# HGRN2 head sums: squared outputs as the moving operand, the rows turned back by four transposes

## The chip, the cores and the metric

The kernel runs on one core of one Trainium2 chip. The metric is the device time of one execution in microseconds (us), median of the runs. The core has a matrix engine (TensorE, PE in the profile, with its weight loads as PEld), VectorE (DVE), ScalarE (ACT), GpSimd (POOL) and SyncE (SP), each with an instruction queue of its own that it works off in order; they wait for each other on semaphores. TensorE writes to PSUM, eight banks of 128 partitions x 512 fp32 values.

## The reference

A trunk of two layers on x of shape (1, 512, 1024), fp32. Each layer is a half-step SwiGLU FFN, a mixer, and a second half-step FFN; a final RMSNorm closes it. The mixer projects the normed input with one matrix W_in, and runs two token mixers side by side, a Mamba-2 SSD head group and an HGRN2 head group, whose outputs W_out joins. The change lies in the norm of the HGRN2 outputs, one for each of the 8 heads of 64 values and each of the 512 tokens:

```
o = (o_intra + o_inter).reshape(Bsz, L, HG_HEADS, HG_VAL_HEAD)
o = o * lax.rsqrt(jnp.mean(o * o, axis=-1, keepdims=True) + NORM_EPS) * norm_w
o = o * jax.nn.silu(g_raw.reshape(Bsz, L, HG_HEADS, HG_VAL_HEAD))
```

So the kernel needs 512 x 8 sums, each over the 64 squares of a head.

## The kernel before, in words

Channels lie on the 128 partitions and the 512 tokens along the free dimension (four tiles of 128 tokens, c = 0 to 3). Large products are made from a high and a low part: for each 128x128 weight block three matmuls of 512 columns (L1215 to L1217, `products`), with the high part of the weights rounded by ScalarE (`whi`) and the low part subtracted by GpSimd (`wlo`, L418). Weight blocks come by DMA from SP into four slots.

In the mixer TensorE goes through the list PROJ, blocks n = 0 to 26 of W_in: f, B, dt, C, then q and i of four head pairs, g0, then xs and z of four head pairs in turn (n = 16 is xs0, 17 z0, 18 xs1, 19 z1, 20 xs2), and g1 to g3. Each block is eight products (k = 0 to 7), that is 24 matmuls, into bank n % 3. The small matmuls of the two mixers are written by hand between the products and behind the blocks. VectorE copies each block out (`evac`) and does most of the elementwise work, ScalarE the exponentials, tanh and squares. The order on each engine is that of the code; there is no planner.

Around the change the order is as follows.

- TensorE: behind the products of n = 18 come the SSD state contributions of pair 0 (`ssd_contribs`, L1461) and `head_sums` (L1491), into bank 7. Then the 24 products of n = 19, then `ssd_outs(0)` (L1477, L1482), which overwrites bank 7 and so waits for `head_norm`, `ssd_turn(1)` (L1445 to L1451), and block n = 20.
- VectorE: `evac(18)` (L812), the convolution of xs1 (L868, L871), its SiLU (L825), `ssd_states(0)` (L1028, L1034), then the wait for `head_sum` and `rsqrt` (L659 to L668), eleven small steps on 128x32 values, the first reading bank 7 and the last signalling `head_norm`. Behind it comes `evac(19)` (L819).
- `head_spreads` (behind n = 20, 22 and 24) uses `rh`, the result, in which tokens lie on partitions and c and head (8c + head) along the free dimension.

In `head_sums` each of the 16 products has a 128x128 tile of squares `km` as its stationary operand and the table `headsum` (128x8 for each head pair p, ones where a channel belongs to a head) as the moving one: 8 columns for each token tile c, accumulated over four pairs.

`acb`, an 8x512 tile, holds the running sums of the SSD decay. Its last reads are in the blocks up to n = 8 (the transposes of `common`, and the splitting into `acb_hi` and `acb_lo`, L1108 and L1110).

Of the kernel before, what the change touches and what calls it, by code (L numbers as in the profile page):

```python
# [23 lines left out]
NP = 4  # L24
# [94 lines left out]
def trunk_kernel(nc, x_in, cols, first_norm, logits, lead, up1, dn1, mix, dtw, up2, dn2, out):  # L119
    ctx = ExitStack()  # L120
    with ctx:
# [3 lines left out]
        def ev(name, per=0, before=0, credit=0):  # L125
            return Event(ctx.enter_context(nc.semaphore(name)), per, before, credit)
# [42 lines left out]
        ident = sb("ident", [P, P])  # L169
# [67 lines left out]
        def bank(i):  # L237
            return ps[:, i, :]
# [70 lines left out]
        o_done = ev("o_done", NP)  # L309
        o_out = ev("o_out", 2 * NP)  # L310
        head_sum = ev("head_sum", 1)
        head_norm = ev("head_norm", 1)
        head_spread = ev("head_spread", NP)
        head_used = ev("head_used", NP)
# [334 lines left out]
        def _(dve):  # L649
# [103 lines left out]
            with dve.Fori(0, DEPTH) as l:  # L753
# [6 lines left out]
                def ready(e, k=0):  # L760
                    dve.wait_ge(e.sem, e.upto(l, k))
# [320 lines left out]
                for n, (kind, pr) in enumerate(PROJ):  # L1082
                    evac(n)
                    if n == 10:
                        ready(cleared)
                    if n == 5:
                        dt_first()
                    if n in (1, 2, 4, 5):
                        gate_f((1, 2, 4, 5).index(n))
                    if kind in ("B", "C"):  # L1090
                        convolve(kind, n)
                    if n == 3:
                        conv_out("B")
                    if kind == "C":
                        dt_rest()
                        conv_out("C")
                        for p in range(NP):
                            scan_f(p)
                    if n == Q0:
                        hg_dist(0)  # L1100
                        hg_q(0)
                    if n == Q0 + 1:
                        dt_out()
                        hg_k(0)
                        hg_tables()
                        hg_levels(0)
                        cb_mask()
                        did(dve.tensor_copy(acb_hi[:], acb[:]))  # L1108
                        settle()
                        made(acb_split, tt(acb_lo[:], acb[:], acb_hi[:].bitcast(F32), ALU.subtract))  # L1110
                    if n in (9, 11, 13):
                        p = (n - 9) // 2
                        if p == 0:
                            ends()
                        hg_dist(p + 1)
                        hg_q(p + 1)
                    if n in (10, 12, 14):
                        p = (n - 10) // 2
                        if p == 0:
                            end_weights()  # L1120
                        hg_mask(p)
                        hg_states(p)
                        hg_k(p + 1)
                        hg_levels(p + 1)
                    if n == 15:
                        ready(proj_out, n)
                        silu(("g", 0), g2[:, 0, :], gs[:, 0, :])
                    if kind == "xs":
                        if pr == 0:
                            hg_mask(3)  # L1130
                            hg_states(3)
                        convolve(pr, n)
                        conv_out(pr)
                        if pr:
                            ssd_states(pr - 1)
                        if pr == 1:
                            ready(head_sum)
                            rsqrt(head_norm, rh, None, bank(7)[:, 0:TC * 8], 1.0 / HALF)
                        if pr == 2:
                            hg_norm(0, 3)  # L1140
                            hg_gate(0)
                            hg_lo(0)
                        if pr == 3:
                            hg_norm(1, 3)
                            group_rsqrt(0)
                    if kind == "z":
                        ready(proj_out, n)
                        silu(("z", pr), g2[:, 0, :], zs[:, pr % 2, :])
                        if pr:
                            ssd_gate(pr - 1)  # L1150
                        ssd_main(pr)
                    if kind == "g" and pr in (1, 2):
                        ready(proj_out, n)
                        silu(("g", pr), g2[:, 0, :], gs[:, pr % 2, :])
                        if pr == 1:
                            ssd_states(3)
                        hg_gate(pr)
                        if pr == 1:
                            ssd_norm(0)
                            ssd_norm(1)  # L1160
                            hg_norm(2, 3)
                            hg_norm(3, 4)
                            hg_lo(1)
                        else:
                            ssd_lo(0)
                            ssd_lo(1)
                            hg_lo(2)
                            ssd_gate(3)
# [30 lines left out]
        def _(pe):  # L1199
# [41 lines left out]
            with pe.Fori(0, DEPTH) as l:  # L1241
                def ready(e, k=0):
                    pe.wait_ge(e.sem, e.upto(l, k))
# [72 lines left out]
                def cols_of(c):  # L1316
                    return slice(c * P, (c + 1) * P)
# [100 lines left out]
                def hg_outs_before_ready(p):  # L1418

                    ready(state, p)  # L1420
                    ready(level, 6 * p + 5)
# [64 lines left out]
                def head_sums():  # L1486

                    ready(o_out, 2 * NP - 1)
                    for c in range(TC):
                        for p in range(NP):  # L1490
                            last = mm(bank(7)[:, 8 * c:8 * c + 8], km[:, p, cols_of(c)], headsum[:, 8 * p:8 * p + 8],  # L1491
                                      start=p == 0, stop=p == NP - 1)
                    last.then_inc(head_sum.sem, 1)

                def head_spreads(p, bk):

# [25 lines left out]
                for i, (n, k0, k1) in enumerate(PBLOCKS):  # L1522
                    w = MIX0 + i
                    ready(split, w)
                    if k0 == 0:
                        ready(proj_out, n - 3)
                    for k in range(k0, k1):
                        norm_steps(1, n, k)
                        if n in (10, 12, 14, 16) and k == SCORES_FROM:
                            hg_scores_ready((n - 10) // 2)  # L1530
                        if n in (11, 13, 15, 17) and k == 6:
                            hg_outs_before_ready((n - 11) // 2)
                        last = products(bank(n % 3), w % NS, k - k0, h_tile(k), k == 0, k == KD - 1)
                        if k == k1 - 1:
                            last.then_inc(blk.sem, 1)

                        if n in (10, 12, 14, 16):
                            for c in SCORES_AT[k]:
                                hg_scores((n - 10) // 2, c)
                        if n in (11, 13, 15, 17) and k == 4:  # L1540
                            hg_outs_inside((n - 11) // 2)
                        if n in (11, 13, 15, 17) and k == 6:
                            hg_outs_before((n - 11) // 2)
                    if k1 < KD:
                        continue
                    if n == 8:
                        common()
                    if n == 9:
                        chunk_ends()
                    if n in (9, 11, 13, 15):  # L1550
                        hg_turn((n - 9) // 2)
                    if n in (10, 12, 14, 16):
                        hg_contribs((n - 10) // 2)
                    if n in (19, 21, 23, 25):
                        ssd_outs((n - 19) // 2)
                    if n in (17, 19, 21, 23):
                        ssd_turn((n - 17) // 2)
                    if n == 22:
                        group_sums(0)
                    if n in (18, 20, 22, 24):  # L1560
                        ssd_contribs((n - 18) // 2)
                    if n == 18:
                        head_sums()
                    if n == 20:
                        head_spreads(0, 3)
                    if n == 22:
                        head_spreads(1, 3)
                    if n == 24:
                        head_spreads(2, 3)
                        head_spreads(3, 4)  # L1570
                        group_spreads(0)
# [112 lines left out]
```

## Time and profile before

| | |
|---|---|
| time, median of 3 runs | 2055.16 us (2054.82 to 2055.25) |
| the profiled execution: time | 2053.32 us |
| its span, first to last instruction | 2051.6 us |
| mean granted clock of TensorE | 0.983 of full speed |
| TensorE busy | 1999.3 us (97%), 10684 matmul records |
| VectorE busy | 811.8 us (40%) |
| ScalarE busy | 660.1 us (32%) |
| GpSimd busy | 850.7 us (41%) |
| DMA | 181.66 MB, mean 89 GB/s |

Busy time is the time in which an engine worked on some instruction. TensorE's matmuls are pipelined, so the distance between the starts of two of them says more than the duration of one. A plain fp32 matmul leaves two records in the profile, a transpose or one of the three matmuls of a product leaves one. The granted clock is the share of TensorE's full 2.4 GHz that the chip gave; it has two levels, 1.0 and 0.5. The mixer of layer 1 lies between about 390 and 620 us of the span, that of layer 2 between about 1400 and 1630 us, and the head sums at 539 and 1547 us.

### The profile page before, as it was taken

How to read it: one execution, taken by the hardware profiler on the slowest of the kernel's cores; microseconds unless marked ns; L12 is line 12 of the kernel's file. 1: busy time of each engine (PE TensorE's matmuls, PEld its weight loads, DVE VectorE, ACT ScalarE, POOL GpSimd, SP SyncE). 2: the span in 40 equal slices, each digit the busy share in tenths (PEclk: the TensorE clock that was granted, in tenths of full speed). 3: DMA queues.
4: the chain of work that ended last, by engine and by line, in shares of the span. 5: the costliest groups of instructions: out<-in, count | busy, mean ns of one | idle time of the engine just before them, and what ended most of it. 6: DMA issues, size and time to landing. Idle time of an engine off the chain costs nothing.

```text
span 2051.6 us, 29158 instructions
## 1 busy us (share of the span) xinstructions
PE 1999.3 (97%) x10684; PEld 1640.8 (80%) x10684; DVE 811.8 (40%) x1274; ACT 660.1 (32%) x903; POOL 850.7 (41%) x362
## 2 busy tenths in 40 slices
PE   8999999979999999999999999999799999999999
PEld 6888888867778888888888888888577788888888
DVE  7222211597786322221142222117868762222112
ACT  4323222343443232323232322224334332322222
POOL 4544445442224344444434444444322244444453
PEclk9999999989999999999999999999899999999998
DMA  4322233221112232233322223322111122223332
GB/s 145 113 100 95 88 104 95 83 73 53 53 61 83 82 102 92 96 93 95 106 94 92 100 93 95 95 87 93 52 63 52 52 93 94 100 93 100 95 94 91
DMA packets 55816, 181.66 MB, mean 89 GB/s; under 512 B 8369, under 2 KB 10417, under 8 KB 55729
## 3 DMA queue, kind: packets, MB, share of 16 engines
q1 hardware_dynamic: 55728, 180.52, 27.1%
q8 instruction: 52, 0.85, 0.2%
q14 instruction: 36, 0.29, 0.0%
HBM read 178.40 MB, written 2.10 MB: 88 GB/s over the span
## 4 chain that ended last, share of the span: by engine, by line
PE 87%; DVE 9%; issue 3%; ACT 1%; DMA 0%; SPq 0%; DVEq 0%; ACTq 0%
PE ps L1215 28%; PE ps L1216 27%; PE ps L1217 27%; DVE acc L832 1%; PE ps L1374 1%; DVE xs L871 1%; DVE lm L1022 0%; DVE b L835 0%; PE ps L1415 0%; PE ps L1491 0%; ACT th L491 0%; PE ps L1230 0%; DVE b L839 0%; DVE t L830 0%; DVE g L819 0%
## 5 line engine op out<-in xcount | busy, mean ns | idle before, releaser
L418 POOL TENSOR_TENSOR wlo<-raw,whi 128x1024 fp32r<-128x1024 f32 x348 | 848.4, 2440 | 1190.0 <-ACT whi L451 626.9
L1215 PE MATMUL ps<-hhi,whi 128*128 128x512 f32 x1840 | 730.5, 397 | 0.0
L1216 PE MATMUL ps<-hlo,whi 128*128 128x512 f32 x1840 | 720.8, 392 | 0.0
L1217 PE MATMUL ps<-hhi,wlo 128*128 128x512 f32 x1840 | 720.5, 392 | 0.0
L1215 PEld LDWEIGHTS ps<-hhi,whi 128*128 128x128 f32 x1840 | 348.9, 190 | 79.8 <-issue 7.2
L1217 PEld LDWEIGHTS ps<-hhi,wlo 128*128 128x128 f32 x1840 | 348.2, 189 | 73.9
L1216 PEld LDWEIGHTS ps<-hlo,whi 128*128 128x128 f32 x1840 | 348.7, 190 | 70.1
L451 ACT ACTIVATE whi<-raw 128x1024 fp32r<-128x1024 f32 x168 | 177.4, 1056 | 358.5 <-PE ps L1217 358.5
L1215 PE MATMUL ps<-ahi,whi 128*128 128x512 f32 x704 | 273.9, 389 | 0.0
L1216 PE MATMUL ps<-alo,whi 128*128 128x512 f32 x704 | 273.9, 389 | 0.0
L1217 PE MATMUL ps<-ahi,wlo 128*128 128x512 f32 x704 | 273.9, 389 | 0.0
L784 DVE TENSOR_TENSOR u<-ps,r 128x512 f32<-128x512 f32 x88 | 60.8, 691 | 387.1 <-PE ps L1217 387.1
L457 ACT ACTIVATE whi<-raw 128x1024 fp32r<-128x1024 f32 x176 | 183.8, 1045 | 28.2 <-PE ps L1217 28.2
L470 ACT ACTIVATE ahi<-u 128x512 f32 (+1 forms) x88 | 55.6, 632 | 405.9 <-DVE u L787 405.9
L794 DVE SCALAR_TENSOR_TENSOR x<-ps,x 128x512 f32<-128x512 f32 x32 | 22.1, 692 | 387.4 <-PE ps L1217 387.4
L1215 PEld LDWEIGHTS ps<-ahi,whi 128*128 128x128 f32 x704 | 132.1, 188 | 27.6
L1216 PEld LDWEIGHTS ps<-alo,whi 128*128 128x128 f32 x704 | 132.1, 188 | 27.4
L1217 PEld LDWEIGHTS ps<-ahi,wlo 128*128 128x128 f32 x704 | 132.1, 188 | 27.3
L466 ACT ACTIVATE g<-g 128x512 f32<-128x512 f32 x88 | 55.5, 631 | 238.7 <-DVE g L782 238.7
L782 DVE TENSOR_TENSOR g<-ps,r 128x512 f32<-128x512 f32 x88 | 60.8, 691 | 177.4 <-PE ps L1217 176.5
L789 DVE TENSOR_TENSOR alo<-u,ahi 128x512 f32 x88 | 63.5, 722 | 83.7 <-ACT ahi L470 83.7
L433 ACT ACTIVATE hhi<-x,par 128x512 fp32r<-128x512 f32 x48 | 34.5, 719 | 150.9 <-DVE x L794 141.6
(225 smaller groups left out, 1389.6 us busy)
## 6 DMA issues: line engine op xcount, KB each, us to landing
raw<-in_up SPq DMA_DIRECT2D x168, 512.0 KB, 3.2
raw<-in_mix SPq DMA_DIRECT2D x66, 512.0 KB, 3.2
raw<-in_dn SPq DMA_DIRECT2D x64, 448.0 KB, 3.3
raw<-in_dn SPq DMA_DIRECT2D x32, 512.0 KB, 3.5
raw<-in_lead SPq DMA_DIRECT2D x12, 512.0 KB, 3.3
stage<-in_x SPq DMA_DIRECT2D x4, 512.0 KB, 7.0
out<-stage SPq DMA_DIRECT2D x8, 256.0 KB, 2.6
raw<-in_mix SPq DMA_DIRECT2D x4, 256.0 KB, 2.5
```

The costliest lines, as they stand in the source:

```text
L418: pool.tensor_tensor(wlo[:, q, :], raw[:, q, :], whi[:, q, :].bitcast(F32), ALU.subtract).then_inc(split.sem, 1)
L433: act.activation(hhi[:, m, :], x[:, m, :], ACT.Copy, scale=gain).then_inc(x_high.sem, 1)
L451: act.activation(whi[:, q, :], raw[:, q, :], ACT.Copy).then_inc(high.sem, 1)
L457: act.activation(whi[:, q, :], raw[:, q, :], ACT.Copy).then_inc(high.sem, 1)
L466: act.activation(g2[:, jj, :], g2[:, jj, :], ACT.Silu).then_inc(silu_g.sem, 1)
L470: act.activation(ahi[:, 2 * i + jj, :], u2[:, jj, :], ACT.Copy).then_inc(hid_high.sem, 1)
L782: made(g_out, tt(g2[:, jj, :], bank(jj), r[:], ALU.mult))
L784: made(u_out, tt(u2[:, jj, :], bank(2 + jj), r[:], ALU.mult))
L789: made(hid_low, tt(alo[:, 2 * i + jj, :], u2[:, jj, :], ahi[:, 2 * i + jj, :].bitcast(F32), ALU.subtract))
L1215: mm(dst, whi[:, q, s], mh, start=start, stop=False)
L1216: mm(dst, whi[:, q, s], ml, start=False, stop=False)
L1217: return mm(dst, wlo[:, q, s], mh, start=False, stop=stop)
```

## The change

The operands of the head sums change places: `headsum` (128x8 for each pair) is the stationary operand and `km`, all 512 tokens of a pair, the moving one. Four products instead of 16 accumulate into rows 0 to 7 of bank 7: heads on partitions, tokens along the free dimension. VectorE copies these 8x512 values to `acb` and signals `head_rows`. TensorE waits for that in block n = 19 ahead of the products k = 3, and behind these products turns the rows by four transposes of 8x128 into bank 7, in the layout of before (`head_turned`). VectorE waits for them and goes on with `rsqrt` as before.

```diff
+        head_rows = ev("head_rows", 1)
+        head_turned = ev("head_turned", 1)
...
                         if pr == 1:
                             ready(head_sum)
+                            made(head_rows, dve.tensor_copy(acb[:], bank(7)[0:8, :]))
+                            ready(head_turned)
                             rsqrt(head_norm, rh, None, bank(7)[:, 0:TC * 8], 1.0 / HALF)
...
                 def head_sums():
 
                     ready(o_out, 2 * NP - 1)
+                    for p in range(NP):
+                        last = mm(bank(7)[0:8, :], headsum[:, 8 * p:8 * p + 8], km[:, p, :],
+                                  start=p == 0, stop=p == NP - 1)
+                    last.then_inc(head_sum.sem, 1)
+
+                def head_turn():
+
                     for c in range(TC):
-                        for p in range(NP):
-                            last = mm(bank(7)[:, 8 * c:8 * c + 8], km[:, p, cols_of(c)], headsum[:, 8 * p:8 * p + 8],
-                                      start=p == 0, stop=p == NP - 1)
-                    last.then_inc(head_sum.sem, 1)
+                        last = pe.transpose(bank(7)[:, 8 * c:8 * c + 8], acb[:, cols_of(c)], ident[0:8, 0:8])
+                    last.then_inc(head_turned.sem, 1)
...
+                        if n == 19 and k == 3:
+                            ready(head_rows)
                         last = products(bank(n % 3), w % NS, k - k0, h_tile(k), k == 0, k == KD - 1)
                         if k == k1 - 1:
                             last.then_inc(blk.sem, 1)
+                        if n == 19 and k == 3:
+                            head_turn()
```

## Rows read from the trace of the kernel before

**Rows 1.** The page, part 4: the chain that ended last, by engine.
```profile
PE 87%; DVE 9%; issue 3%; ACT 1%; DMA 0%; SPq 0%; DVEq 0%; ACTq 0%
```

**Rows 2.** The chain of waits, layer 1: start us, us, what.
```profile
539.07 3.75 PE ps L1491 x32
...
544.30 0.43 PE ps L1215
...
558.89 0.24 PE ps L1217
```

**Rows 3.** Timeline of TensorE, layer 1: start us, us, engine, line, operation.
```profile
538.20 0.87 PE L1461 MATMUL ps<-xde,bt 128*64 128x128 f32 x6
539.00 3.82 PE L1491 MATMUL ps<-headsum,km 128*128 128x8 f32 x32
542.68 0.78 PE L1215 MATMUL ps<-hhi,whi 128*128 128x512 f32 x1
...
549.54 0.39 PE L1217 MATMUL ps<-hhi,wlo 128*128 128x512 f32 x1
```

**Rows 4.** Timeline of VectorE, layer 1; in brackets idle time before, and its releaser.
```profile
539.39 2.69 DVE L868 TENSOR_SCALAR xs<-xr,par 128x512 f32<-128x512 f32 x1
...
547.02 0.17 DVE L659 TENSOR_SCALAR ntn<-ps 128x32 f32<-128x32 f32 x1
...
550.06 0.69 DVE L819 SCALAR_TENSOR_TENSOR g<-ps,r 128x512 f32<-128x512 f32 x1 [0.61 <-PE ps L1217]
...
557.73 1.28 DVE L1022 TENSOR_TENSOR lm<-lm,cbm 128x512 f32<-128x512 f32 x2
...
559.89 0.55 DVE L868 TENSOR_SCALAR xs<-xr,par 128x512 f32<-128x512 f32 x1
```

**Rows 5.** Timeline of TensorE, layer 2.
```profile
1546.73 4.55 PE L1491 MATMUL ps<-headsum,km 128*128 128x8 f32 x32
...
1558.88 0.39 PE L1217 MATMUL ps<-hhi,wlo 128*128 128x512 f32 x1
```

**Rows 6.** Timeline of VectorE, layer 2.
```profile
1554.74 0.18 DVE L659 TENSOR_SCALAR ntn<-ps 128x32 f32<-128x32 f32 x1
```

**Rows 7.** Stretches: start:end, us, TensorE busy (records), granted clock, DMA share, GB/s.
```profile
542.52:545.94 3.42, 3.42 (x10) 0.50 0.47 153
617.62:621.03 3.41, 3.41 (x10) 0.50 0.45 138
1549.45:1556.28 6.83, 6.83 (x22) 0.50 0.26 79
1624.55:1631.37 6.82, 6.82 (x25) 0.50 0.24 77
```

**Rows 8.** Operations from PSUM by line (ns min/median/max); transposes on the timeline of TensorE.
```profile
L703 DVE COPY r<-ps x6: 692/692/692, 41.0 to 1685.1; 128x512 f32<-128x512 f32 x6
...
L810 DVE TENSOR_TENSOR dtb<-ps,r x2: 671/672/672, 412.3 to 1420.7; 8x512 f32<-8x512 f32 x2
...
530.63 0.39 PE L1217 MATMUL ps<-hhi,wlo 128*128 128x512 f32 x1
530.86 0.60 PE L1445 MATMUL ps<-ident,xs 128*128 128x128 f32 x4
531.39 0.49 PE L1450 MATMUL ps<-acb_hi,identr 8*128 8x512 f32 x1
...
435.13 0.59 PE L1327 MATMUL ps<-ident,dtb 8*128 8x8 f32 x4
```

**Rows 9.** Waits of TensorE, 530 to 625 us (total, times, longest); one on the timelines.
```profile
PE ps L1477 <- DVE st L1034: 2.6, 2, 1.5
PE ps L1513 <- ACT sqb L491: 1.7, 1, 1.7
...
1575.84 0.96 DVE L1034 SCALAR_TENSOR_TENSOR st<-st,u,ps 64x64 f32<-64x64 f32 x4
...
1576.86 1.09 PE L1477 MATMUL ps<-lm,xdt 128*64 128x128 f32 x16 [1.06 <-DVE st L1034]
```

## The prediction

> **What bounds the kernel now.** I read the page first, then the chain of waits around the head sums, then the timelines of TensorE and VectorE there, in both layers. The page puts 87% of the chain of work that ended last on TensorE [rows 1], so the question in each stretch is whether TensorE may go on. In the chain of waits the sums themselves stand with 3.75 us, the products of block n = 19 (z1) behind them, and TensorE still at the last product of n = 20, which ends at 559.13 [rows 2]. So TensorE holds the end right through the place that is changed: whatever delays the last product of n = 19 delays everything behind it.
>
> The timeline of layer 1 [rows 3] gives the path. The 32 records of the sums start at 539.00, the 24 products of n = 19 run from 542.68 to 549.54 (last start). In layer 2 [rows 5] the sums start at 1546.73 and the last product at 1558.88. The granted clock is half (1.2 GHz) just behind the sums: for 3.4 us in layer 1 and 6.8 us in layer 2 [rows 7]. At that level successive 128x512 products are 0.43 us apart [rows 2], at 2.4 GHz 0.23 us (530.63 to 530.86 [rows 8]). That is why layer 2 needs longer for the same work.
>
> VectorE is the second path. In layer 1 it convolves block n = 18 (one pass of it takes 2.69 us), forms the SSD states and starts the head square root at 547.02, 4.4 us after TensorE had its sums ready (32 x 0.1117 us behind 539.00) [rows 3, 4]. The square root ends at 549.45, 0.61 us ahead of the next copy out at 550.06. In layer 2 the square root starts at 1554.74 [rows 6]. Today TensorE needs nothing of this before the end of n = 19, and its products fill the time.
>
> **The change part by part.** *The sums.* Before, 16 products give 32 records, 0.1117 us apart (3.57 us, to 542.57; the first product follows at 542.68) [rows 3]. After, four products of 512 columns give 8 records. No row shows a 512-column product of plain fp32. The nearest is the state contribution, fp32 with 128 columns: six records in 0.87 us, of which the last one's own 0.27 us run past the others' starts, so (0.87 - 0.27) / 5 = 0.12 us apart, 0.11 without the slower first [rows 3]; four times the columns make 0.44 us, and 8 records 3.5 us. The lower bound is the 0.23 us of a 512-column product of the other form, 8 x 0.23 = 1.8 us; the upper is the half clock, 7.0 us. I take 3.5 us: no gain to speak of in time. What may change is the clock, since the array now streams full-length operands instead of 8 columns.
>
> *The new wait.* TensorE waits for head_rows in front of the products k = 3 of n = 19. VectorE makes head_rows by a copy that stands, in its order, behind the convolution of n = 18 and behind the SSD states. It can't start before 547.02 in layer 1 and 1554.74 in layer 2, the present starts of the square root, since nothing ahead of it on VectorE depends on the sums. The copy reads 8x512 from PSUM. A 128x512 copy from PSUM takes 0.69 us and an 8x512 operation from PSUM 0.67 us [rows 8], so eight partitions are no cheaper than 128; the lowest bound is the 0.17 us of the 128x32 step [rows 4]. I take 0.69, and 0.06 us to wake TensorE (VectorE's states end at 1575.84 + 0.96 = 1576.80, the outputs that waited for them start at 1576.86 [rows 9]). TensorE goes on at 547.77 and 1555.49.
>
> When does it get there? In layer 1 at full clock: sums to 542.5, first product at 542.7, nine products (the first behind another kind of work takes 0.11 us more, 0.49 against 0.39 us [rows 8], so one pitch of 0.34, then 0.23) last start 544.65, streaming over at about 544.9. So it stands still for 2.9 us; the same sum gives 2.9 us in layer 2 (1546.73 + 3.5 + 0.2, nine products, 1552.6, against 1555.49). Behind the waiting product are 15 products of n = 19, and behind those the SSD outputs, the turning of x, and by way of the block's semaphore ScalarE's rounding of the next weights, GpSimd's subtraction and SP's next load. All move together; weights lie split ahead, so none of them is a new wait.
>
> *The four transposes.* Group L1445 shows what four transposes between long products cost: from the product at 530.63 to the one at 531.39 is 0.76 us, where 0.23 is usual, and the pitch after it is 0.34 instead of 0.23 [rows 8]. Together 0.64 us. The eight-row ones in the trace (x4 in 0.59 us, against 0.60) are not cheaper [rows 8].
>
> *End of n = 19.* Restart + 0.34 + 0.23 + 0.76 (over the transposes) + 0.34 + 10 x 0.23 = restart + 3.97 us. Layer 1: 547.77 + 3.97 = 551.74 against 549.54, **+2.2 us**. Layer 2: 1555.49 + 3.97 = 1559.46 against 1558.88, **+0.6 us** (it was already late, for its 6.8 us of half clock). Without the transposes and the copy the stall alone would still be there; they are not the cause but 0.64 + 0.69 us of it per layer.
>
> *The square root moves too.* It now starts when the transposes end, about 549.15, and needs 547.02 to 549.45 = 2.43 us [rows 4], so it ends at 551.6; the copy out of n = 19 would come at 551.74 + 0.52 = 552.26 (0.52 as from 549.54 to 550.06 [rows 3, 4]). That covers it by 0.65 us. If that cover goes, each further us is one on the path, as the SSD outputs wait for head_norm. Is the delay won back later? From the copy out of n = 19 (550.06) VectorE works, tied to that block by the tanh, until 559.0, and TensorE's last product of n = 20 ends at 559.13 [rows 2, 4]: both paths start at the end of n = 19 and are as long, so the delay goes through whole. Sum at full clock: **+2.8 us**.
>
> *The clock behind the stall.* In layer 1 TensorE stood idle for up to 1.5 us in front of the SSD outputs and the clock did not fall; it stood idle 1.7 us in front of the group sums, which are one-column products, and it fell for 3.4 us at 617.62; the like place of layer 2 has 6.8 us at 1624.55 [rows 7, 9]. The new stall of 2.9 us is longer than each of them, with five full products and four short transposes behind it. So I expect a fall. In a stretch of 3.4 us at the low level 8 products start where 15 would: 1.6 us lost, for each layer. The before times hold their own falls, since I compare with their real ends. The Trainium skill (Perfetto Trace Analysis, Matmul Optimizations) says that TensorE's power scales with utilization, so that matmuls should run back to back in batches. The falls above agree; by that rule the stall costs more than its length, and without it the sum would stay at the full-clock one.
>
> Sum with a fall in both layers: 2.8 + 2 x 1.6 = **+6.0 us**. The durations are of the profiled execution, 2053.32 us with a span of 2051.6; the median of the runs shown is 2055.16, 1.84 more, and I put the difference on the median: 2061.2 us.
>
> **The rivals.**
> 1. *A fall in one layer only.* Where the stall lies against the clock's decisions is chance, and an idle time of 1.5 us passed [rows 9]. +4.4 us: 2059.6.
> 2. *No fall behind the stall,* or the fall comes right behind the sums as now (eight columns of weights may count for as little as eight columns of data) and is spent in the nine products and the stall: nine at 0.43 us end by 546.6, still ahead of 547.77. +2.8 us: 2058.0. For it: both sums of before were followed by a fall [rows 7]. Against: there the data were 8 columns wide.
> 3. *Not slower: VectorE is early.* The long pass of the convolution in n = 18 takes 2.69 us beside a subtraction on GpSimd; the same pass in n = 20 takes 0.55 us [rows 4]. Should the two no longer meet, the copy starts 2.14 us sooner, TensorE restarts at 545.63 and 1553.35, and n = 19 ends at 549.60 and 1557.32: +0.06 - 1.56 = -1.5 us, 2053.7. It decides from 2.1 us on. The skill (Advanced Engine Details and Errata, VectorE Performance Modes) says that two-port VectorE instructions and GpSimd's block each other; the trace agrees (2.69 against 0.55). Against it: both instructions are released by the end of n = 18's products, ahead of the first changed instruction, in both layers.
> 4. *The long sums are slow* (half clock during and after, 7.0 us): TensorE reaches the wait at 546.2 + nine products at 0.43 = 550.1, 2.4 us behind 547.77, in both layers: 2.8 + 4.8 = +7.6, with a little of the low stretch behind it about +8.5: 2063.7.
>
> **How the numbers follow.** Fall in both layers 0.43, in one 0.27, none 0.19, VectorE early 0.05, slow sums 0.06. What a measurement of this kernel can tell from no change is 0.2%, 4.1 us: faster by more than that has no case of its own, only the last rival's sign with shifted clock stretches elsewhere (0.04); within 0.2% are the case without a fall, VectorE early, and a part of the one-fall case, whose +4.4 is at the edge (0.32); slower 0.64. Range: from 2058.0 less 1.0 (a copy of 0.17 us in both layers) to the slow-sum case: 2057.0 to 2063.8.
>
> **What would show it.** In the profile after: L1491's successor with 8 records of about 0.44 us; a stall of TensorE of 2 to 3 us in n = 19 released by VectorE's copy to acb, in both layers; the copy at 0.6 to 0.7 us starting at the time of today's first square-root step; the last product of n = 19 at +2.2 to +3.8 us in layer 1; half clock in the stretch after the stall. It would be wrong if TensorE doesn't wait for head_rows, if VectorE reaches its copy more than 2 us sooner, or if later stages take the delay up.

## The result, and the profile after

| | before | after |
|---|---|---|
| median | 2054.95 us (20 runs, 2050.59 to 2057.08) | 2058.27 us (20 runs, 2056.29 to 2065.32) |
| the profiled execution: time, span | 2053.32, 2051.6 us | 2065.32, 2063.6 us |
| granted clock in it | 0.983 | 0.982 |

The ratio is 1.0020, 95% interval 1.0013 to 1.0026: the change makes the kernel slower, by 2.7 to 5.3 us (the medians differ by 3.3). The profiled execution of the changed kernel is the slowest of its 20, so its span overstates the loss; its rows show the mechanism, the medians the size.

The page of the changed kernel. TensorE is still the chain; the new entry is in the last row: in front of the bracket are busy time and mean ns, behind it the idle time of TensorE before this line, 6.2 us, of which VectorE's write of `acb` ends 5.7.

```profile
span 2063.6 us, 29080 instructions
...
PE 86%; DVE 10%; issue 3%; ACT 1%; DMA 0%; SPq 0%; DVEq 0%; ACTq 0%
...
L1219 PE MATMUL ps<-hhi,whi 128*128 128x512 f32 x1840 | 732.2, 398 | 6.2 <-DVE acb L1140 5.7
```

TensorE in layer 1, the answer to [rows 2, 3] (start us, us, line, operation, in brackets idle time before and what ended it):

```profile
538.33 0.87 PE L1465 MATMUL ps<-xde,bt 128*64 128x128 f32 x6
539.13 3.60 PE L1494 MATMUL ps<-km,headsum 128*8 128x512 f32 x8
542.66 0.50 PE L1219 MATMUL ps<-hhi,whi 128*128 128x512 f32 x1
...
544.62 0.39 PE L1221 MATMUL ps<-hhi,wlo 128*128 128x512 f32 x1
547.87 0.50 PE L1219 MATMUL ps<-hhi,whi 128*128 128x512 f32 x1 [2.87 <-DVE acb L1140]
548.21 0.59 PE L1220 MATMUL ps<-hlo,whi 128*128 128x512 f32 x1
548.60 0.63 PE L1221 MATMUL ps<-hhi,wlo 128*128 128x512 f32 x1
549.16 0.59 PE L1501 MATMUL ps<-ident,acb 8*128 8x8 f32 x4
549.68 0.80 PE L1219 MATMUL ps<-hhi,whi 128*128 128x512 f32 x1
...
553.23 0.39 PE L1221 MATMUL ps<-hhi,wlo 128*128 128x512 f32 x1
553.55 1.09 PE L1481 MATMUL ps<-lm,xdt 128*64 128x128 f32 x16
```

The sums are 8 records in 3.60 us where 32 took 3.82, and the first product behind them starts at 542.66, before at 542.68. The whole stage lies 0.13 us later here. After nine products it stands still for 2.87 us. Then the distance from 548.21 to 548.60 is already 0.39 and from 548.60 to 549.16 0.56: the clock has fallen. The last product of n = 19 starts at 553.23; before, at 549.54.

VectorE there, against [rows 4]:

```profile
547.15 0.67 DVE L1140 COPY acb<-ps 8x512 f32<-8x512 f32 x1
549.79 0.19 DVE L661 TENSOR_SCALAR ntn<-ps 128x32 f32<-128x32 f32 x1 [1.97 <-PE ps L1501]
...
552.04 0.20 DVE L670 SCALAR_TENSOR_TENSOR rh<-ntn,rh 128x32 f32<-128x32 f32 x1
553.75 0.69 DVE L821 SCALAR_TENSOR_TENSOR g<-ps,r 128x512 f32<-128x512 f32 x1 [1.51 <-PE ps L1221]
```

The copy starts at the time at which the square root started before (547.15, with the whole stage 0.13 later), then VectorE waits 1.97 us for the transposes. The square root is over at 552.24, 1.51 us ahead of the copy out of n = 19: it is hidden.

TensorE in layer 2, against [rows 5]: the same stall to the hundredth.

```profile
1552.53 3.60 PE L1494 MATMUL ps<-km,headsum 128*8 128x512 f32 x8
...
1561.27 0.50 PE L1219 MATMUL ps<-hhi,whi 128*128 128x512 f32 x1 [2.87 <-DVE acb L1140]
...
1562.27 0.59 PE L1501 MATMUL ps<-ident,acb 8*128 8x8 f32 x4
...
1566.96 1.09 PE L1481 MATMUL ps<-lm,xdt 128*64 128x128 f32 x16
```

Stretches at half clock (start:end, us, busy, granted clock, DMA share, GB/s), against [rows 7]. The first two stand right behind the two stalls. Those at 619.91 and 1637.09 take the place of the ones at 617.62 (3.41 us) and 1624.55 (6.82 us) before. Those at 1606.37 and 1688.29 had no counterpart before.

```profile
548.24:551.65 3.41, 3.41 (x12) 0.50 0.00 0
1562.00:1565.40 3.40, 3.40 (x12) 0.50 0.02 5
619.91:626.74 6.83, 6.83 (x21) 0.50 0.22 77
1637.09:1640.50 3.41, 3.41 (x10) 0.50 0.39 127
1606.37:1613.19 6.82, 6.82 (x17) 0.50 0.23 77
1688.29:1695.11 6.82, 6.82 (x20) 0.50 0.14 57
```

Measured from the start of the state contributions (538.20 and 538.33 in layer 1, 1545.93 and 1551.73 in layer 2), the last product of n = 19 starts 11.34 and 12.95 us behind them in the kernel before, and 14.90 and 14.90 us in the changed one. So the changed place costs 3.56 + 1.95 = 5.5 us in this execution. The other 6.5 us of the 12.0 between the spans lie elsewhere: 1.6 at the end of the first mixer (half clock for 6.83 us at 619.91 in place of 3.41), 0.5 between the mixers, 3.1 in the second, where the 6.82 us at 1606 fall, 2.1 less at its end (3.41 us at 1637.09 in place of 6.82), 3.2 behind it, where those at 1688 fall, and 0.1 ahead of it all.

The stretch at 1606 matters, since the prediction took its place for safe. It begins 1.9 us behind the restart from an idle time that the kernel before has too, there without a fall. The same instruction before and after:

```profile
1596.67 1.09 PE L1477 MATMUL ps<-lm,xdt 128*64 128x128 f32 x16 [1.52 <-DVE st L1034]
1604.42 1.09 PE L1481 MATMUL ps<-lm,xdt 128*64 128x128 f32 x16 [1.51 <-DVE st L1036]
```

### The profile page after: what moved, and what is told of

It reads as the page before. It is cut to its first block, busy times and chain, and to the rows that moved or that the text cites. A ratio compares the mean times of both kernels' runs of the same rounds, so it can differ in the third digit from the quotient of the medians.

```text
span 2063.6 us, 29080 instructions
## 1 busy us (share of the span) xinstructions
PE 2005.1 (97%) x10644; PEld 1637.1 (79%) x10644; DVE 815.7 (40%) x1276; ACT 660.0 (32%) x903; POOL 850.0 (41%) x362
## 4 chain that ended last, share of the span: by engine, by line
PE 86%; DVE 10%; issue 3%; ACT 1%; DMA 0%; SPq 0%; DVEq 0%; ACTq 0%
PE ps L1219 27%; PE ps L1221 27%; PE ps L1220 27%; DVE acc L834 1%; PE ps L1378 1%; DVE xs L873 1%; ACT th L493 0%; DVE lm L1024 0%; DVE b L837 0%; PE ps L1419 0%; DVE xs L870 0%; DVE g L821 0%; PE ps L1234 0%; DVE b L841 0%; DVE t L832 0%
```

## The experiments

Each ratio is against the kernel before of the same session. "TensorE's wait" is for the copy in block n = 19; in e5 it is for the square root, in front of the SSD outputs, and stands outside the last column. "Sums to end" is the time from the state contributions to the last product of n = 19, layer 1 and layer 2, in the profiled execution; before it is 11.34 and 12.95.

| run | median us | ratio (95%) | TensorE's wait, us | sums to end |
|---|---|---|---|---|
| the change again | 2057.22 | 1.0018 (1.0009 to 1.0026) | 2.9 | 16.36, 14.89 |
| e1 copy early | 2051.28 | 0.9988 (0.9979 to 0.9997) | 0.3 | 10.85, 10.88 |
| e2 stall alone | 2054.18 | 1.0006 (0.9997 to 1.0015) | 0.6, 0.3 | 15.04, 13.31 |
| e3 work alone | 2052.48 | 0.9993 (0.9983 to 1.0003) | none | 10.25, 10.25 |
| e4 stall filled | 2055.59 | 1.0012 (1.0003 to 1.0021) | filled | 13.39, 13.39 |
| e5 wait at k = 7 | 2070.75 | 1.0088 (1.0075 to 1.0102) | 4.7 (root) | 10.10, 10.11 |
| e6 copy before the states | 2055.13 | 1.0013 (1.0004 to 1.0022) | 1.7 | 12.19, 12.20 |

Before was 2054.28 in the session of the first four, 2052.82 in that of the last three.

**The change again.**

> The changed kernel again, beside the runs of the kernel before of the same session, as the base for the others. Every theory: +2.5 to +4.5 us against before (2058.27 against 2054.95 so far). In the profile TensorE stands 2.9 us at k = 3 of n = 19 in both layers. What is open is the clock: if the stall is what lets it fall, half-clock stretches follow the stall in most executions.

Measured 1.0018, with 2.9 us of wait in both layers. The loss repeats. The profiled execution, 2061.62 us, is again the slowest, here of 11.

**The copy early (e1).**

```diff
                         convolve(pr, n)
+                        if pr == 1:
+                            ready(head_sum)
+                            made(head_rows, dve.tensor_copy(acb[:], bank(7)[0:8, :]))
                         conv_out(pr)
...
-                            ready(head_sum)
-                            made(head_rows, dve.tensor_copy(acb[:], bank(7)[0:8, :]))
```

> The copy of the eight rows stands right behind the convolution of xs1, in VectorE's idle time for ScalarE's tanh (0.78 us), in place of behind the SSD states. Stall theory: the copy runs from 544.5 to 545.2 (layer 1), TensorE's stall shrinks from 2.9 to about 0.3 us, the transposes are done before VectorE asks for them, the square root starts at 547.0 as before, and the SSD outputs follow at about 549.6 (before 549.86) and, without the half clock behind the sums, 1.9 us earlier than before in layer 2: 0.3 to 4 us faster than before, 2 to 6 faster than the change. Rival, the added work itself costs (four transposes, the copy, long fp32 products): still 2 us or more slower than before.

VectorE and TensorE in layer 1:

```profile
544.48 0.68 DVE L1137 COPY acb<-ps 8x512 f32<-8x512 f32 x1
545.22 0.69 DVE L827 SCALAR_TENSOR_TENSOR xs<-th,xs 128x512 f32<-128x512 f32 x1
...
547.03 0.18 DVE L661 TENSOR_SCALAR ntn<-ps 128x32 f32<-128x32 f32 x1
```

```profile
539.02 3.60 PE L1495 MATMUL ps<-km,headsum 128*8 128x512 f32 x8
...
545.22 0.50 PE L1220 MATMUL ps<-hhi,whi 128*128 128x512 f32 x1 [0.32 <-DVE acb L1137]
...
549.61 1.09 PE L1482 MATMUL ps<-lm,xdt 128*64 128x128 f32 x16
```

The copy lies in the gap in which VectorE waited for ScalarE's tanh, and the SiLU behind it starts at 545.22, as it did at 545.21 before. TensorE waits 0.32 us, and the SSD outputs start at 549.61. The ratio is below one and its interval too: the same arithmetic, with one instruction of VectorE elsewhere, beats the kernel before by 0.6 to 4.3 us, and the changed kernel too. That the added work costs 2 us is refuted. Layer 2 gives most, since no half clock follows the sums there (before, 6.83 us [rows 7]).

**The stall alone (e2).** Old sums, no transposes; the copy is a dummy.

```diff
+                            made(head_rows, dve.tensor_copy(acb[:], bank(7)[0:8, :]))
                             rsqrt(head_norm, rh, None, bank(7)[:, 0:TC * 8], 1.0 / HALF)
...
+                        if n == 19 and k == 3:
+                            ready(head_rows)
```

> The sums stay as in the kernel before (16 products of 8 columns, no transposes); only VectorE's copy of 8x512 behind the SSD states is added (its values are not used) and TensorE's wait for it at k = 3 of n = 19. Stall theory: almost all of the loss comes with it: restart at the same time as in the changed kernel, last product 0.64 us earlier per layer, so +1.5 to +3.5 us against before. The work theory: near nothing, 0 to +0.7 us.

Measured 1.0006. The interval, -0.6 to +3.1 us, holds the forecasts of both theories (+1.5 to +3.5, and 0 to +0.7), so the time decides nothing. The trace says more; TensorE in layer 1:

```profile
539.20 4.08 PE L1493 MATMUL ps<-headsum,km 128*128 128x8 f32 x32
543.13 0.77 PE L1217 MATMUL ps<-hhi,whi 128*128 128x512 f32 x1
...
546.69 0.63 PE L1219 MATMUL ps<-hhi,wlo 128*128 128x512 f32 x1
547.94 0.80 PE L1217 MATMUL ps<-hhi,whi 128*128 128x512 f32 x1 [0.62 <-DVE acb L1139]
...
553.77 1.09 PE L1479 MATMUL ps<-lm,xdt 128*64 128x128 f32 x16
```

With the old sums the clock falls before they are over, the nine products start 0.43 us apart and TensorE reaches the wait only at 547.3, where it stands 0.62 us for the copy. It goes on 9.54 us behind the state contributions (547.94 - 538.40), and in the changed kernel too (547.87 - 538.33): the copy sets the restart, whether the time before it is filled by slow products or idle. The new sums only bring TensorE to the same wait 2.3 us sooner. So the block ends 3.7 and 0.4 us later than before in this execution. Its span is still only 0.7 us longer (2052.3 against 2051.6), because two stretches of half clock of before are missing here: 3.4 us at 669 and 6.8 us at 1625, the latter in [rows 7]. TensorE gains 1.7 and 3.1 us there. Why they are missing is not shown, and so this run does not price the wait alone.

**The work alone (e3).** The transposes turn `dtb`, long finished, so copy and wait fall away.

```diff
-                            made(head_rows, dve.tensor_copy(acb[:], bank(7)[0:8, :]))
                             ready(head_turned)
...
-                        last = pe.transpose(bank(7)[:, 8 * c:8 * c + 8], acb[:, cols_of(c)], ident[0:8, 0:8])
+                        last = pe.transpose(bank(7)[:, 8 * c:8 * c + 8], dtb[:, cols_of(c)], ident[0:8, 0:8])
...
-                        if n == 19 and k == 3:
-                            ready(head_rows)
```

> The new sums and the four transposes stay, but the transposes turn another 8x512 tile that is long finished, so VectorE's copy and TensorE's wait fall away (the head norm is computed from wrong values; the work is the same). Stall theory: no stall in n = 19, end of the block at about 549.5, 0.3 us (layer 1) to 1.9 us (layer 2) earlier than before: 0.3 to 4 us faster than before. Work theory: as slow as the change, +2.5 to +4 us.

```profile
538.65 3.60 PE L1493 MATMUL ps<-km,headsum 128*8 128x512 f32 x8
...
545.14 0.41 PE L1500 MATMUL ps<-ident,dtb 8*128 8x8 f32 x4
...
549.25 1.09 PE L1480 MATMUL ps<-lm,xdt 128*64 128x128 f32 x16 [0.76 <-DVE rh L670]
```

The sums are as long as in the change, the transposes are there, the clock stays at 1.00 in the whole stage in both layers, and TensorE ends n = 19 after 10.25 us and waits 0.76 us for the square root. The ratio, 0.9993, is not clear of one but is clear of the change's. Sums and transposes without the wait don't make the kernel slower; the block ends after 10.25 us, where it took 11.34 and 12.95 with the half clock at the sums.

**The stall filled (e4).** Dense work in place of idleness, same restart.

```diff
                         if n == 19 and k == 3:
+                            ready(xdt_made, 0)
+                            for _ in range(12):
+                                mm(bank(3), whi[:, w % NS, 0:P], hhi[:, 0, :], start=True, stop=True)
                             ready(head_rows)
```

> The changed kernel with 12 more 128x512 matmuls (into a bank that is free there, their result is not used) ahead of the wait at k = 3 of n = 19, some 2.8 us of dense work where TensorE stood idle. The restart stays where it was, as VectorE's copy sets it. If the half clock behind the stall is a part of the loss: no half-clock stretch behind it, and 1 to 3 us faster than the change, so +0.5 to +2.5 against before. If the clock has no part in it: as slow as the change (+3 to +4), or a little slower.

```profile
544.25 0.39 PE L1221 MATMUL ps<-hhi,wlo 128*128 128x512 f32 x1
544.47 2.88 PE L1545 MATMUL ps<-hhi,whi 128*128 128x512 f32 x12
547.50 0.50 PE L1219 MATMUL ps<-hhi,whi 128*128 128x512 f32 x1
...
551.68 1.09 PE L1481 MATMUL ps<-lm,xdt 128*64 128x128 f32 x16
```

Block n = 19 ends after 13.39 us in both layers, with no half clock on the way. The prediction's full-clock sums were 551.74 - 538.20 = 13.54 and 1559.46 - 1545.93 = 13.53. The ratio is 1.0012 against the change's 1.0018 and 1.0020, which would put the clock's part at 1 to 2 us; by the medians (+2.8 us against +2.9 and +3.3) it is 0.2 to 0.6. The intervals overlap, so the timed runs don't show that it is above zero. Only the traces do, for the profiled executions: 13.39 against 14.9 or more.

**The wait at k = 7 (e5).** Both the wait and the transposes moved to the last product of n = 19 (`k == 3` to `k == 7`).

> The wait and the four transposes stand at k = 7 of n = 19 in place of k = 3. TensorE comes to the wait at about 547.6, as the copy ends (547.8), so it doesn't stall there; but the square root starts only when the transposes end (about 548.9) and ends at 551.3, and the SSD outputs wait for it. Stall theory, in which VectorE's copy, TensorE's turn and VectorE's root are one serial chain: end of that chain at about 551.4 in place of 552.1 (end of the block in the change at full clock): +1 to +3 against before, the stall of 1.5 us now in front of the SSD outputs. If only the place of the wait were at fault: no slower than before.

The direction was right and the size badly wrong: about +18 us where 1 to 3 were expected. TensorE in front of the SSD outputs, then VectorE and GpSimd, then the clock:

```profile
549.10 0.41 PE L1501 MATMUL ps<-ident,acb 8*128 8x8 f32 x4
554.23 1.98 PE L1481 MATMUL ps<-lm,xdt 128*64 128x128 f32 x16 [4.72 <-DVE rh L670]
```

```profile
549.55 0.19 DVE L661 TENSOR_SCALAR ntn<-ps 128x32 f32<-128x32 f32 x1 [1.39 <-PE ps L1501]
...
550.21 0.19 DVE L668 TENSOR_TENSOR ntn<-ntn 128x32 f32<-128x32 f32 x1
550.44 2.29 DVE L670 SCALAR_TENSOR_TENSOR rh<-ntn,rh 128x32 f32<-128x32 f32 x1
552.76 0.19 DVE L666 SCALAR_TENSOR_TENSOR ntn<-rh 128x32 f32<-128x32 f32 x1
```

```profile
550.34 2.34 POOL L420 TENSOR_TENSOR wlo<-raw,whi 128x1024 fp32r<-128x1024 f32 x1 [8.09 <-ACT whi L453]
```

```profile
552.23:565.88 13.65, 11.65 (x48) 0.50 0.10 39
1569.40:1583.00 13.60, 11.73 (x49) 0.50 0.12 39
```

TensorE does not stall in n = 19, but the square root now runs from 549.55, into GpSimd's subtraction at 550.34. One of its steps, 128x32, takes 2.29 us in place of 0.19. TensorE is idle for 4.72 us, and the clock stays at half for 13.65 us, in layer 2 alike (13.60). So k = 3 was not at fault; the serial chain of copy, turn and root is, and the place at k = 3 had hidden its last link.

**The copy before the states (e6).** As e1, but behind `conv_out(pr)`.

> VectorE's copy stands behind the SiLU of xs1 and ahead of the SSD states: 1.2 us sooner than in the change, 1.5 us later than in the version with the copy behind the convolution. Stall theory: TensorE's stall is 1.7 us (2.9 and 0.3 in the other two), so the time lies between them: about 1.2 us sooner per layer than the change, 0 to +1.5 against before; the head square root starts 0.7 us later than before, when VectorE has done the copy and the states. Rival, that a longer stall is free until the clock falls: as the early copy, -2 to -3.

The wait of TensorE (total, times, longest):

```profile
PE ps L1220 <- DVE acb L1138: 1.7, 1, 1.7
```

Wait 1.7 us, sums to end 12.19 and 12.20: at full clock each us by which the copy is later is a us of the block (10.85 with 0.3, 12.19 with 1.7, 13.39 with 2.9 filled). The ratio of 1.0013 (+0.8 to +4.5 us) is not what these would give, 0.85 later and 0.75 earlier than before, and more than the 0 to +1.5 expected, though the interval touches that. In its profiled execution 6.8 us of half clock fell at 590 and at 1600, where before has none. Both begin 1.8 to 2.0 us behind the restart from 1.51 us of idle time in front of SSD outputs, as the one at 1606 in the changed kernel does. Why there, was not tried.

**The clock in further executions.**

> The changed kernel, one more profiled execution. Open is how often the half clock follows the stall on TensorE's path. Forecast of the record: in both layers (end of n = 19 about 14.9 us behind the state contributions); if the stall is as often followed by none, some layers show 13.4 us, as with the filled stall.

> As the look before it: 13.4 us from the state contributions to the last product of n = 19 without a half-clock stretch on the path, 14.9 with one of 3.4 us, 16.4 with one of 6.8 us.

> The kernel before, one more profiled execution: the half clock directly behind the sums in both layers, 3.4 or 6.8 us long, and 11.3 or 12.9 us from the state contributions to the last product of n = 19. If the sums don't always bring it, one layer shows less than 11 us.

The two further executions of the changed kernel (2062.96 and 2060.45 us) had sums to end of 14.88 and 14.88, and 16.39 and 14.90; that of before (2053.37 us) 11.35 and 11.36. In the four profiled executions of the changed kernel half clock comes at the end of all eight stalls or right behind (3.4 us in six, 6.8 in two). With the sums of before (two executions of that kernel, one of e2) it falls 2.7 to 3.5 us behind the start of the sums, ahead of the first product, in six layers of six; with the long sums and no wait over 1.7 us in the block (e1, e3, e4, e6) there is none before the SSD outputs in eight of eight.

One thing more stands in these traces. All four of the changed kernel have the 6.8 us of half clock at about 1605 us, behind 1.5 us of idle time in front of the SSD outputs; neither of the two of before has it. In the twelve traces together such an idle time comes 24 times and is followed by 6.8 us of half clock 7 times: these four, e3 in layer 1, and e6 in both. In the first execution it costs 3.1 us, as much as the two falls behind the stalls together (2 x 1.5, against e4).

## Why the prediction was right, and where its size was off

- *TensorE holds the end, VectorE sets the restart.* Right. Copy at 547.15 for 0.67 us, restart at 547.87, stall 2.87 us in both layers, and the same 9.54 us from state contributions to restart in e2, with other sums in front. Forecast: 0.69, 547.77 (with the stage 0.13 earlier), 2.9.
- *Sums: no gain in time.* Right: 3.60 us against 3.5 forecast; e3 and e1 show them free. The half-clock rival (slow sums) didn't occur.
- *Transposes 0.64 us.* Slightly high at full clock: in e4 the product ahead of them and the one behind are 0.66 us apart (548.08 to 548.74), where 0.76 was forecast, and that is most of the 0.15 us between 13.39 and 13.54.
- *Square root hidden.* Right in the change; e5 shows what happens without this cover. The prediction said that each further us would be one on the path; it was more, since GpSimd's subtraction and the clock came on top.
- *End of n = 19 at full clock, +2.8 us in all.* Right: e4 has 13.39 against 11.34 and 12.95, so +2.05 + 0.44 = +2.5 us, and as a ratio 1.0012, +2.5 us.
- *The clock, 2 x 1.6 us.* The mis-sized term, and the step that took the forecast to nearly double the measured loss. Each profiled execution has the fall in both layers (+3.56 and +1.95 in the first, forecast 3.8 and 2.2). But the medians are 3.3 and 2.9 us above before, not 6.0. Of the 31 timed executions of the changed kernel 8 have a mean granted clock of 0.984 or less and take 2059.3 us or more; the other 23 have 0.985 to 0.988 and take 2055.9 to 2059.6. Those of e4, which has no fall there, have 0.986 to 0.988. The median granted clock is even higher than before: 0.986 and 0.987, against 0.984 and 0.985 for the kernel before in the two sessions that list it. That fits executions in which the fall at the sums is gone and none has come in its place, and the rival of no fall, 2058.0, names the median better than the forecast's 2061.2. The four traced executions take 2060.45 us and more, as only 5 of the 31 do, so the traces show the minority. It is not shown where the half clock lies in the others, nor why all traced ones have it behind the stall. This stays open. The measured time lies in the range because that reaches down past this rival; the case with the highest chance missed by 2.9 us.
- *The clock behind shorter idle times.* The prediction reasoned from 1.5 us in front of the SSD outputs that passed without a fall, and put no term there. All four traced executions of the changed kernel have a fall behind just such a time in layer 2, worth 3.1 us in the first. Like the other falls, it is not shown for the median.
- *The base.* Before varies too, from 2049.60 to 2057.08; its own falls at the sums differ from one trace to the other (6.8 or 3.4 us in layer 2), though that these make the spread is not shown. The forecast took the one execution with 6.8 us in layer 2 as the rule and 1.84 us between it and the median as a constant.
- *VectorE early.* The rival waited for VectorE to be 2.14 us sooner by chance and priced that at -1.5 us. It can be had by order: in e1 the copy starts 2.6 us sooner, and the ratio is 0.9988, -2.5 us.

## What to carry to other kernels

Turning 16 short products into four long ones gains nothing if the new hand-over goes through an engine whose queue is behind: read first when that queue reaches the new instruction, and put it into a gap it already has, here the wait for a tanh. Where another queue sets the restart, making the work in front of the wait faster only makes the wait longer, as e2 and the change with the same restart show. A chain that crosses two engines and back wants its last link looked at too, against what the other engines run beside it (e5). And a few traces of one kernel may all show the same falls of the clock and still not stand for the median: compare the granted clock of the timed executions first.

## What the runs showed of the hardware

- Plain fp32 with 512 columns: two records of 0.43 us a product (eight records from 539.13, next product at 542.66), four times the 0.11 us of 128 columns [rows 3], with only 8 columns of weights.
- The clock fell in the course of 3.6 us of gapless 8-column products in all six layers traced. In the eighteen layers with the long sums it fell in none before the next idle time. What in the short sums brings it is not shown: their weights differ too. The Trainium skill (Perfetto Trace Analysis, Matmul Optimizations) ties the power of the engine to its utilization and asks for matmuls back to back. The falls behind the stalls agree; those in the short sums come while TensorE is busy without a gap, so that rule alone does not tell the two forms apart.
- Idle times of TensorE and the half clock: at the end of 2.9 us or right behind it came in eight of eight layers of the changed kernel, behind 1.67 us in e6 in neither of two (none before the SSD outputs), behind 1.5 us in front of the SSD outputs in 7 of 24, and during the 4.72 us of e5 in both.
- A 128x32 VectorE step next to a GpSimd subtraction took 2.29 us in place of 0.19 (e5). The Trainium skill (Advanced Engine Details and Errata, GPSIMD Details) lists VectorE instructions with two SBUF inputs among those that conflict with GpSimd's; this step has two. The page gives no size there; here so short a step took nearly as long as the whole subtraction of 2.34 us.
- A VectorE copy of 8x512 from PSUM takes 0.67 us, of 128x512 0.69 [rows 8].
